# Second mixer of a two-block transformer: computed between the tiles of its input projection instead of behind it

## The reference, cut to what matters

```python
h = rmsnorm(x, mix_pre_gain)                      # 256 x 2048
proj = h @ w_in_2                                 # 2048 x 5376
q_a, k_a, v_a, q_r, f_r, i_r, g_r = split(proj)   # 1024,128,128,1024,1024,1024,1024
attn = rmsnorm(sliding_window_attention(q_a, k_a, v_a, sinks), attn_out_gain)  # 16 heads of 64, 2 key heads
f = lb + (1 - lb) * sigmoid(f_r); key = 1 - f; q = silu(q_r); v = i_r          # 8 heads of 128
b = cumsum(log f)
att[t, s] = sum_k q[t,k] key[s,k] exp(b[t,k] - b[s,k])   for s <= t
o = att @ v;  o = o * rsqrt(mean(o*o) + EPS) * norm_gain * silu(g_r)
mixed = concat(attn, o) @ w_out_2                 # 2048 x 2048
```

## Time and profile before

| | |
|---|---|
| median of 3 runs | 2506.15 us (2505.97 to 2507.98) |
| the profiled execution, time | 2511.62 us |
| its span | 2509.8 us |
| TensorE busy | 2386.6 us of the span |
| VectorE busy | 1453.9 us |
| ScalarE busy | 1155.2 us |
| mean granted TensorE clock | 0.977 of full |
| input projection of block 2 (from the span's start) | 1285.1 to 1516.1 us |
| mixer of block 2, its last transposes included | 1516.1 to 1683.8 us |
| output projection of block 2 | 1683.8 to 1771.8 us |

### The profile page before, as it was taken

The page is one execution under the profiler, slowest core; times in us unless marked ns, Lnnn a source line. Parts: engine busy times, 40 slices in busy tenths (PEclk is TensorE's granted clock), DMA queues, the critical chain, the costliest instruction groups (busy, mean ns, idle before and its releaser), DMA issues.

```text
span 2509.8 us, 34138 instructions
## 1 busy us (share of the span) xinstructions
PE 2386.6 (95%) x12062; PEld 1992.9 (79%) x12062; DVE 1453.9 (58%) x1806; ACT 1155.2 (46%) x1619; POOL 38.7 (2%) x61
## 2 busy tenths in 40 slices
PE   6999977999999999999999997869999999999997
PEld 5888856888888888888878885658888888888886
DVE  4444467557777546776554445975566544566544
ACT  4444335455555444555444445444444444444432
POOL 1000100000000000000000000000000000000000
PEclk9999878999999999999999998979999999999999
DMA  7666341646556666556666651016566666656663
GB/s 234 189 190 183 99 143 42 193 139 190 183 178 195 192 192 186 177 187 210 185 201 190 190 162 47 1 45 192 142 201 185 191 190 190 190 184 184 209 192 101
DMA packets 298804, 418.97 MB, mean 167 GB/s; under 512 B 15439, under 2 KB 181657, under 8 KB 297957
## 3 DMA queue, kind: packets, MB, share of 16 engines
q1 hardware_dynamic: 295744, 407.09, 53.2%
q0 software_dynamic: 2400, 8.68, 1.1%
q10 hardware_dynamic: 580, 2.20, 0.2%
HBM read 415.80 MB, written 2.12 MB: 167 GB/s over the span
## 4 chain that ended last, share of the span: by engine, by line
PE 80%; DVE 7%; issue 7%; ACT 2%; DMA 2%; POOL 0%; DVEq 0%; SPq 0%; POOLq 0%; ACTq 0%
PE PS L1346 22%; PE PS L1313 15%; PE PS L1314 15%; PE PS L1312 14%; PE PS L1347 11%; PE PS L1364 1%; DVE x L979 1%; DMA root_rows<-small 1%; DVE proj L1246 1%; DVE proj L1235 1%; ACT work L704 1%; DVE fackf L1242 1%; DMA stage<-in_w_in 1%; DMA root_row<-root_rows 1%; DVE work L1090 1%
## 5 line engine op out<-in xcount | busy, mean ns | idle before, releaser
L835 DVE TENSOR_TENSOR wlo<-stage,whi 128x1024 fp32r<-128x1024 f32 (+2 forms) x452 | 540.6, 1199 | 614.9 <-ACT whi L537 614.8
L1346 PE MATMUL PS<-actT,whi 128*128 128x512 f32 x2432 | 861.4, 398 | 3.0 <-DVE wlo L864 3.0
L537 ACT ACTIVATE whi<-stage 128x1024 fp32r<-128x1024 f32 (+2 forms) x452 | 468.6, 1038 | 671.1 <-PE PS L1314 646.0
L1347 PE MATMUL PS<-actT,wlo 128*128 128x256 f32 x2432 | 684.2, 281 | 0.0
L1346 PEld LDWEIGHTS PS<-actT,whi 128*128 128x128 f32 x2432 | 458.0, 188 | 116.9 <-DVE wlo L864 3.6
L864 DVE TENSOR_TENSOR wlo<-stage,whi 128x1024 fp32r<-128x1024 f32 x298 | 362.8, 1223 | 238.2 <-ACT whi L598 238.1
L598 ACT ACTIVATE whi<-stage 128x1024 fp32r<-128x1024 f32 x298 | 315.9, 1061 | 321.3 <-PE PS L1347 307.5
L1347 PEld LDWEIGHTS PS<-actT,wlo 128*128 128x128 f32 x2432 | 457.2, 188 | 0.1
L1313 PE MATMUL PS<-wlo,actT 128*128 128x512 f32 (+2 forms) x992 | 383.6, 387 | 0.0
L1312 PE MATMUL PS<-whi,actT 128*128 128x512 f32 (+2 forms) x992 | 383.6, 387 | 0.0
L1314 PE MATMUL PS<-whi,actT 128*128 128x512 f32 (+2 forms) x992 | 380.5, 384 | 0.0
(11 more groups left out here) (263 smaller groups left out, 1481.4 us busy)
## 6 DMA issues: line engine op xcount, KB each, us to landing
stage<-in_w_up SPq DMA_DIRECT2D x304, 512.0 KB, 3.9
stage<-in_w_down SPq DMA_DIRECT2D x216, 512.0 KB, 4.5
stage<-in_w_in SPq DMA_DIRECT2D x168, 512.0 KB, 4.5
stage<-in_w_out SPq DMA_DIRECT2D x64, 512.0 KB, 4.7
stage<-in_cmp_k_w SPq DMA_DIRECT2D x8, 512.0 KB, 4.6
stage<-in_cmp_v_w SPq DMA_DIRECT2D x8, 512.0 KB, 5.8
x<-in_x ACTq DMA_DIRECT2D x2, 1024.0 KB, 6.9
grow<-bias_by_distance POOLq DMA_DIRECT2D x2, 1024.0 KB, 7.5
```

The costliest lines, as they stand in the source:

```text
L537: nc.scalar.activation(whi[:, s % SPLITS, 0:wd], stage[:, s % STAGES, 0:wd], ACT.Copy)\
L835: nc.vector.tensor_tensor(wlo[:, s % SPLITS, 0:wd], stage[:, s % STAGES, 0:wd], whi[:, s % SPLITS, 0:wd].bitcast(F32), ALU.subtract).then_ ...
L1346: nc.tensor.matmul(o, whi[:, j % SPLITS, at], actT[:, k, :], start=k == 0, stop=False)
L1347: last = nc.tensor.matmul(o[:, S:2 * S], wlo[:, j % SPLITS, at], actT[:, k, 0:S], start=False, stop=k == KC - 1)
```

## The change

The 88 tiles of `in2` are written out one by one, in the order of `IN2_BLOCKS`: keys and values first, then the window queries feature-major, half of the RNN values token-major, forget gates and RNN queries feature-major in turn, then the other half of the values and the gates. 12 blocks of 4 tiles are feature-major (48 tiles), 5 token-major (40 tiles, the first 8 of them half as wide). Queries and forgets thus arrive as the transposes left them before; only the doubled keys (4 transposes) and the logarithms (two groups of 8) are still transposed.

Between these tiles stand the 16 window heads (`WINDOW_AT`, ahead of tiles 25 to 43) and the 16 steps (`STEP_AT`, ahead of tiles 57 to 82), each cut into pieces at fixed distances: on TensorE scores at n, turn at n + 2, values at n + 3; exponents at n, levels at n + 2, `att @ v` at n + 4. The projection uses PSUM banks 0 to 3, the mixer 4 to 7 (and bank 1 for `att @ v`). `qf` and `kf` get two buffers. The diagonal comes out of the level products: `keep` also takes u == t where t is the last of the lower half of a level, and the one missing corner, token 127, comes from a 32 x 32 product. `cross_out` moves from ScalarE to VectorE. The mean squares are split in two halves. The transposes for `out2` run in pairs of chunks: 4 chunks ahead of tile 87, 8 behind it, 4 between tiles 5 and 6 of `out2`, which is also written out instead of looped.

```diff
+IN2_BLOCKS = [("tok", C_KA, 256)] + [("feat", C_QA + 256 * i, 256) for i in range(4)] + [("tok", C_IR, NW)]
+for _i in range(4):
+    IN2_BLOCKS += [("feat", C_FR + 256 * _i, 256), ("feat", C_QR + 256 * _i, 256)]
+IN2_BLOCKS += [("tok", C_IR + NW, NW), ("tok", C_GR, NW), ("tok", C_GR + NW, NW)]
+IN2_BANKS = [(2 * (k % 2), 2 * (k % 2) + 1) for k in range(14)] + [(0, 3), (2, 0), (3, 2)]
+WINDOW_AT = {25 + 5 * s // 4: s for s in range(HA)}
+STEP_AT = {n: r for r, n in enumerate((57, 59, 60, 62, 63, 65, 66, 68, 72, 73, 75, 76, 78, 79, 81, 82))}
...
-        keep[:, n, :] = same & (u % (2 * ln) < ln) & (t % (2 * ln) >= ln)
+        keep[:, n, :] = same & (u % (2 * ln) < ln) & (t % (2 * ln) >= ln) | (u == t) & (t % (2 * ln) == ln - 1)
-    keep[:, 7, :] = u == t
+    keep[P - 1, 0, P - 1] = 1.0
...
 # ScalarE
+            def low_sums2(k):
+                act.wait_ge(ev("tile_used"), used(G["in2"].first + IN2_FIRST[k] + 4))
+                nc.scalar.activation(feat_dst(k), PS[:, b:b + 2, S:2 * S], ACT.Copy, ...).then_inc(ev("in2_low"), 1)
...
+            for n in range(AHEAD, IN2_TILES + AHEAD):
+                act.wait_ge(ev("tile_used"), used(G["in2"].first + n - SPLITS + 1))
+                act.wait_ge(ev(f"landed{n % STAGES}"), 16 * ((G["in2"].first + n) // STAGES + 1))
+                nc.scalar.activation(whi[:, n % SPLITS, 0:wd], stage[:, n % STAGES, 0:wd], ACT.Copy).then_inc(ev("hi_done"), 1)
...
+                ended = in2_end(n - 3)
+                if ended in FEAT_NO: low_sums2(ended)
+                if ended in TOK_NO: tokens_out(ended)
+                if n - 5 in WINDOW_AT: window_turned(WINDOW_AT[n - 5])
+                if n - 4 in WINDOW_AT: window_exp(WINDOW_AT[n - 4])
+                if n == 50: attention_squares()
+                if n - 3 in STEP_AT: decays(STEP_AT[n - 3])
+                if n - 7 in STEP_AT: o_out(STEP_AT[n - 7])
+                if n in (52, 68): sigmoids(n // 68)
+                if n in (54, 70): logs(n // 70)
+                if n in (57, 73): logs_turned(n // 73)
+                if n in (86, 90): gate_sigmoid(n // 90)
...
 # VectorE
+            def join2(k):
+                dve.wait_ge(ev("in2_low"), i + 1)
+                nc.vector.scalar_tensor_tensor(to, PS[:, b:b + 2, 0:S], ..., to, ALU.mult, ALU.add).then_inc(ev("in2_join"), 1)
+                dve.wait_ge(ev("row_in"), 32)
+                dve.wait_ge(ev("in2_join"), i + 1)
+                nc.vector.tensor_tensor(to, to, row, ALU.mult).then_inc(ev("in2_feat"), 1)
...
+            for n in range(AHEAD, IN2_TILES + AHEAD):
+                dve.wait_ge(ev("hi_done"), G["in2"].first + n + 1)
+                nc.vector.tensor_tensor(wlo[:, n % SPLITS, 0:wd], ..., ALU.subtract).then_inc(ev("lo_done"), 1)
+                if n == 7: root_of_x(3, 6)
+                if in2_end(n - 3) in FEAT_NO: join2(in2_end(n - 3))
...
+                if n - 6 in WINDOW_AT: take_out2(WINDOW_AT[n - 6])
+                if n - 4 in WINDOW_AT: weigh2(WINDOW_AT[n - 4])
+                if n - 3 in WINDOW_AT: front2(WINDOW_AT[n - 3])
+                if n in (52, 68): forgets(n // 68)
+                if n in (55, 71): keys(n // 71)
+                if n - 5 in STEP_AT: attention_levels(STEP_AT[n - 5])
+                if n - 3 in STEP_AT: products(STEP_AT[n - 3])
...
+            split_turned("mix2", range(8), MIX2_BANK)
+            gated(1)
+            split_turned("mix2", range(8, 12), MIX2_BANK)
+            tok("out2", False, then_first="up2a", beside=last_chunks)
...
 # TensorE
+            for n in range(IN2_TILES):
+                if n == 19: key_turn()
+                if n - 3 in WINDOW_AT: window_values(WINDOW_AT[n - 3])
+                if n - 2 in WINDOW_AT: window_turn(WINDOW_AT[n - 2])
+                if n in WINDOW_AT: window_scores(WINDOW_AT[n])
+                if n in (54, 70): logs_turn(n // 70)
+                if n - 4 in STEP_AT: values(STEP_AT[n - 4])
+                if n - 2 in STEP_AT: levels(STEP_AT[n - 2])
+                if n in STEP_AT: exponents(STEP_AT[n])
+                if n == IN2_TILES - 1:
+                    for p in range(2): turn_mix2(p)
+                in2_tile(n)
+            for p in range(2, 6): turn_mix2(p)
...
+            def last_turned(j):
+                if j == 6:
+                    for p in (6, 7): turn_mix2(p)
+            tok("out2", actT, turned="mix2", between=last_turned)
```

More of the change, by code:

```diff
@@ L555, in take @@
                     for t in range(TT):
[L556 to L557 removed]
+                        last = nc.scalar.activation(dst[:, t, span(col, wd)], PS[:, 4 * g.turned + 2 * bank + t, 0:wd], ACT.Copy)
                     last.then_inc(ev("acc_free"), 1)
@@ L792, in _ @@
-            decays(0)
-            for n in range(NR + 3):
-                window_turned(n)
-                if 1 <= n <= NR and (n - 1) % TT == 1:
-                    cross_out((n - 1) // TT)
-                if n >= 3:
-                    o_out(n - 3)
-                if n + 1 < NR:
-                    decays(n + 1)
-                window_exp(n)
-            first_tiles("out2")
-            act.wait_ge(ev("o_out2"), HA)
-            act.wait_ge(ev("o_out"), NR)
-            for t in range(TT):
-                last = nc.scalar.activation(squares[t][:, 0:1024], proj2[:, t, C_QA:C_QA + 1024],
-                                            ACT.Square, accum_out=small[:, t:t + 1])
@@ L808, in _, with tokens_out @@
-            last.then_inc(ev("ssq"), 1)
-            split_turned("mix2")
-            tok("out2", "squares", then_first="up2a")
+            def low_sums2(k):
+                b = IN2_BANKS[k][0]
+                act.wait_ge(ev("tile_used"), used(G["in2"].first + IN2_FIRST[k] + 4))
+                nc.scalar.activation(feat_dst(k), PS[:, b:b + 2, S:2 * S], ACT.Copy,
+                                     scale=64 ** -0.5 if FEAT_NO[k] < 4 else 1.0).then_inc(ev("in2_low"), 1)
+            def tokens_out(k):
+                act.wait_ge(ev("rstd"), 6)
+                for t in range(TT):
+                    if t == 0 and k >= 14:
+                        act.wait_ge(ev("first_half"), k - 13)
+                    else:
+                        act.wait_ge(ev("tile_used"), used(G["in2"].first + IN2_FIRST[k] + 8))
+                    nc.scalar.activation(tok_dst(k)[:, t, :], PS[:, IN2_BANKS[k][t], 0:IN2_BLOCKS[k][2]], ACT.Copy,
+                                         scale=small[:, 4 + t:5 + t]).then_inc(ev("in2_tok"), 1)
@@ L811, in _, with last_chunks @@
+            def last_chunks(j):
+                if j == 2:
+                    split_turned("mix2", range(12, KC), MIX2_BANK)
+            split_turned("mix2", range(12), MIX2_BANK)
+            tok("out2", "squares", then_first="up2a", beside=last_chunks)
             split_turned("n4")
@@ L1298, in one @@
                     for j in range(T):
+                        if between is not None and b == 0:
+                            between(j)
                         if turned is not None and b == 0:
@@ L1318, in tok @@
                     pe.wait_ge(ev("g_lo"), G[up].acc + G[up].blocks)
+                if between is not None:
+                    pairs = 0
                 if pairs:
@@ new lines, in _ @@
+            for n in range(IN2_TILES):
+                if n == 19:
+                    key_turn()
+                if n - 3 in WINDOW_AT:
+                    window_values(WINDOW_AT[n - 3])
+                if n - 2 in WINDOW_AT:
+                    window_turn(WINDOW_AT[n - 2])
+                if n in WINDOW_AT:
+                    window_scores(WINDOW_AT[n])
+                if n in (54, 70):
+                    logs_turn(n // 70)
+                if n - 4 in STEP_AT:
+                    values(STEP_AT[n - 4])
+                if n - 2 in STEP_AT:
+                    levels(STEP_AT[n - 2])
+                if n in STEP_AT:
+                    exponents(STEP_AT[n])
+                if n == IN2_TILES - 1:
+                    for p in range(2):
+                        turn_mix2(p)
+                in2_tile(n)
```

698 lines of the change are left out of this document (421 added, 277 removed).

## The result

The changed kernel takes 2495.56 us in the median of 4 runs (2494.21 to 2496.12), the kernel before beside it 2507.07 (2505.97 to 2511.18). The ratio is 0.9937, 95% interval 0.9924 to 0.9950: 11.5 us faster by the medians and 15.8 by the ratio, where 37.5 were forecast. The direction is right, and the time lies above the range. The profiled execution of after took 2494.21 us with a span of 2492.4, 17.4 less than the span before. From the first tile of `in2` (1283.9) to the last of `out2` (1754.9) it needs 471.0 us: 486.7 before, 449.2 forecast. So 21.8 us of the stage have to be found. One run of experiment 7 took 2663.81 us at a granted clock of 0.842 (its other four 2486.86 to 2495.52); it is in that kernel's median and not in its ratio.

The account below looks back on a forecast made before the run. TensorE, busy 95% of the span, was taken as the bound, the mixer being a VectorE stage between its projections. Stage: 351.8 + 97.4 = 449.2 us against 486.7, 37.5 less, giving 2469 us; range 2441 to 2492.

Parts of the forecast that it names:

- TensorE at clock 1.00 throughout: Sign expected in the profile after: TensorE keeps its full granted clock from `in2` to the end of `out2`.
- rival 3: Some 20 scattered waits drop the woven stage's clock to the mixer's mean 0.87: +51 us, kernel 2520; chance 0.05.
- a corner of 32 columns replaces the diagonal: In each step's levels, a diagonal of 32 columns instead of 128 saves about 0.1 us of TensorE.
- Ends of blocks among the heads: ScalarE's copies of finished blocks delay the heads' exp at tiles 31, 35, 39, 43: TensorE waits 2.6, 1.4, 2.0, 2.0 us.
- `exponents(2)` ahead of tile 60: TensorE waits 1.9 us for `fac`, because `decays(1)` stands behind a block's low sums on ScalarE.
- The masks at tiles 62, 65 and 81: Single PSUM level banks make `levels(r)` wait for the previous step's mask on VectorE: 1.6, 2.3 and 1.7 us.
- Tiles 67 and 68: Sigmoids and `forgets` stand ahead of masks and products of steps 4 and 5: TensorE waits 0.9 + 2.0 + 1.5 us.
- The end: Splits ready 4.8 us after tile 87, transposes filling 1.9; some 3.7 us lost at tile 6 of `out2`.
- The root row: Transfer for `join2` of the first feature block, arriving about 1313.4, stays hidden behind tiles 12 to 14 by 1.5 us.
- Rival 1: Queues absorb the waits: 21 us of waits and 6 of the end vanish, kernel 2441; chance 0.20.
- Rival 2: VectorE's order costs double, every step waiting like those at 65 to 68: 25 us more, kernel 2494; chance 0.17.
- Rival 4: Nothing comes of the change: 37 us more waits, by the root row or a starved instruction stream; chance 0.03.

Follow-up runs that it names:

- experiment 7: Changed kernel with `o_out` ahead of `decays` on ScalarE: 2490.24 us, ratio 0.9909 to the kernel before.
- experiment 5: Changed kernel with late low-sum, token and join copies, late forget gates, and earlier splits and transposes at the end: 2457.05 us, ratio 0.9784.
- Experiment 1: Changed kernel, same order, with 99 identity products of 128 x 128 filling TensorE's waits at ten places: 2482.01 us, ratio 0.9883.
- experiment 10: experiment 5 with four deliberate TensorE pauses ahead of tiles 9, 13, 17 and 21, waiting for a later tile's split: 2472.23 us, ratio 0.9846.
- experiment 6: Kernel before the change, its two long mixer pauses filled with small products (54, then 14 and 26): 2507.50 us, ratio 0.9984.
- experiment 9: experiment 5 plus one 128 x 128 product ahead of each of tiles 8 to 24, 17 in all: 2462.88 us, ratio 0.9818.
- Experiment 2: Changed kernel with `low_sums2` and `tokens_out` behind the heads' and steps' work on ScalarE, `join2` behind `front2` on VectorE: 2479.17 us, ratio 0.9871.
- experiment 3: Changed kernel with `forgets` at n = 52 and 68 behind `attention_levels` and `products` on VectorE: 2490.54 us, ratio 0.9913.
- Experiment 4: Changed kernel with the first 4 chunks split during tile 87, last transposes ahead of `out2` tile 5, their split two tiles later: 2485.18 us, ratio 0.9889.
- 8: experiment 5 plus `o_out` ahead of `decays` on ScalarE: 2459.92 us, ratio 0.9791.

## Why the prediction was wrong

The stage, as TensorE spends it, in us. The columns of after and of experiment 5 add up, by line, the time from the start of each product to the start of the next, less the waits.

| | forecast | after | experiment 5 |
|---|---|---|---|
| 48 feature-major tiles | 135.8 | 145.9 | 138.3 |
| 40 token-major tiles | 99.1 | 103.7 | 103.5 |
| 16 heads and 16 steps | 92.8 | 99.2 | 93.5 |
| transposes | 5.9 | 5.9 | 5.4 |
| `out2` | 88.0 | 89.7 | 88.1 |
| waits | 27.6 | 26.5 | 6.7 |

The forecast column adds up to 449.2 (its steps' waits, named one by one, to 12.3 where the sum has 12.4), the last one to 435.5, and the trace of experiment 5 has 1723.1 - 1287.5 = 435.6. That of after adds up to 470.9 for 471.0.

**The step that failed** is "TensorE at clock 1.00 throughout", and the sentence behind it in rival 3: "the old loop idled 12% in pieces and kept 1.00; the clock fell where idle time was 17.6 of 28 us; my longest wait is under 5". I priced each wait at its length. The pieces of the old loop were 0.5 and 0.8 us long, as the one in the earlier trace rows; mine were 1 to 6. Waits of 1.07, 1.81, 2.14 and 2.47 us were each followed by 1.2 GHz. What it cost is the difference between the last two columns without the waits: 7.6 + 0.2 + 5.7 + 0.5 + 1.6 = 15.6 us. Experiment 1, with the order unchanged, shows 15.9 less in the same rows (428.5) and won 13.6 by filling the same waits; experiment 10 shows the mechanism alone. Rival 3 was the right mechanism with a size too large: 34.1 us of low clock are 0.07 of the stage, not the 0.26 taken from the mixer's mean, and before and after differ little in low time (44.4 and 34.1 us). What differs is what TensorE does in it. Before, it is mostly idle (experiment 6: 34 us less of it are worth 4); after, it is dense work.

The Trainium skill ("TensorE: Matmul & The Clock Gate", A second HAM failure mode) says that short idle times between groups of products let the clock swing between its two levels. Experiment 1 agrees. The page has the median product at its full-clock duration and puts the loss between the bursts; here most products keep theirs too, but those in the stretches take 0.64 us a pair, and the loss lies in them.

**The term that was too small** is TensorE's own work at full clock: 138.3 + 103.5 + 93.5 in experiment 5 against 135.8 + 99.1 + 92.8, 7.6 us. The prediction named it ("if the woven groups cost more TensorE time beside fp32r tiles than among themselves") and took nothing for it. By the starts some 5.1 us of it stand on the first fp32r product behind each of 54 groups, 0.08 to 0.12 a time; experiment 9 shows that this is the end of the last float32 pass and not yet a price of mixing. What can be read is inside a group. The prediction took 0.1 off a step because a corner of 32 columns replaces the diagonal. Levels, corner (line 1818) and the next exponents in experiment 5:

```profile
1478.41 1.72 PE L1815 MATMUL PS<-win 128*128 128x128 f32 x14
1480.07 0.25 PE L1818 MATMUL PS<-QRT,FRT 128*32 128x32 f32 x2
1480.25 1.12 PE L1801 MATMUL PS<-grow,logf 128*128 128x512 f32 x2
1481.21 0.81 PE L1802 MATMUL PS<-grow,logf 128*128 128x384 f32 x2
```

Levels and corner take 1480.25 - 1478.41 = 1.84 us, and the pair of exponents behind the corner 0.96 instead of 0.86 (1484.90 to 1485.76, the next exponents, which stand behind an fp32r tile): together 1.94 against 1.79 for levels and diagonal in the prediction. The corner costs 0.15 more where 0.1 less was forecast: 0.25 x 16 = 4.0 us. The 8 half-wide tiles took 11.6 instead of 11.1. The other 3.1 us stay open. All of this is read from traces; no run isolates the corner.

Together 15.6 + 7.6 - 0.4 (transposes and `out2`) - 1.1 (waits) is 21.7, the difference of the two columns. The medians differ less than the profiled pair, 11.5 against 17.4 us: the profiled execution before lay 4.5 over its median, that of after 1.4 under.

**The waits, place by place.**
- Ends of blocks among the heads, 8.0 forecast: 2.47 + 1.07 + 1.81 + 1.81 = 7.2. Experiment 2 removed all by the order of the copies, so their cause is right.
- `exponents(2)` ahead of tile 60, 1.9: 1.60, and gone with the low sums. Right.
- The masks at tiles 62, 65 and 81, 5.6 in all: only 0.77, at 62. In their place stand 2.14 at tile 64 and 2.37 at tile 80, ahead of `att @ v`. I had the chain over the mask and its single banks; the one that ended last was `o_out` of the step before, queued on ScalarE behind `decays`. Experiment 7 shows it, by what went and by what came. That the steps' waits still add up, 12.8 for 12.4, is in part luck.
- Tiles 67 and 68, 4.4: 5.95 at 67. The start is as forecast (`forgets` ahead of masks and products, experiment 3), the way to TensorE again over `o_out`. ScalarE and VectorE of after:

```profile
1545.96 1.28 ACT L862 ACT_TABLE_LOAD   x1 [5.40 <-DVE win L1351]
1547.25 1.02 ACT L862 ACTIVATE win<-PS 128x1024 f32<-128x1024 f32 x1
1548.17 0.27 ACT L867 ACTIVATE logf<-PS 128x128 f32<-128x128 f32 x1
1548.33 0.29 ACT L868 ACTIVATE PS<-PS 128x128 f32<-128x128 f32 x1
```

```profile
1539.96 1.38 DVE L1303 TENSOR_SCALAR FRT<-FRT,lbs 128x256 f32<-128x256 f32 x4
1541.26 1.08 DVE L1363 TENSOR_TENSOR win<-PS,grow 128x896 f32<-128x896 f32 x1
...
1543.64 1.22 DVE L1344 TENSOR_TENSOR win<-win,QRT 128x1024 f32<-128x1024 f32 x1
1544.77 1.08 DVE L1351 TENSOR_TENSOR win<-win,FRT 128x896 f32<-128x896 f32 x1
```

  ScalarE stands in `decays(6)` until VectorE has the products of step 5, loads the table, takes the exp, and only then reaches the `o_out` that TensorE waits for. The table load is on the path here, 1.28 of the 5.95: it came after ScalarE's wait, not in it as in the earlier trace rows. The Trainium skill ("ScalarE: Activation LUTs", What ACT_TABLE_LOAD costs) has a drain beside the load; none stands in these rows either.
- The end, 2.9 and 3.7: 3.03 and 3.52. Experiment 4 removed both.
- The root row, hidden by 1.5 us: hidden. VectorE waited 4.86 us for it, and TensorE not at all:

```profile
1312.93 0.69 DVE L1279 TENSOR_TENSOR win<-win,root_row 128x512 f32<-128x512 f32 x1 [4.86 <-DMA root_row<-root_rows]
```

**The rivals.** Rival 1 (the queues absorb the waits, 2441) did not hold for this order, but experiment 5 comes near it by another order: 2457, short by 6.7 us of waits and 7.6 of TensorE's own time. Rival 2 gives 2494 and so nearly the measured time, by a mechanism that did not happen: VectorE's order did not cost double. Without experiments the time alone would have spoken for it. Rival 4 is out.

## What to carry to other kernels

A wait of 1 to 6 us in a dense stream of TensorE has to be priced at its length and at what may then be done at 1.2 GHz: here seven of eleven places were followed by a low stretch, at about 2 us each (15.6 in all), and removing 8.8 us of waits won 16.6. When independent work is woven between tiles, the copies that nobody waits for go behind the work that TensorE waits for, in every queue; here that order (experiments 2 and 3) and the earlier end were worth more than twice the change itself. Low clock is a cost only where TensorE has work: compare not how much there is, but what lies in it.

## What the runs showed of the hardware

- At seven of the eleven places where TensorE waits in the changed kernel the granted clock was 0.5 for 3.41 or 6.83 us; at the others, one of them 3.03 us long, it stayed at 1.00. The same wait of 1.63 us was followed by a low stretch in experiments 9 and 10 and not in 2, 5 and 8. The length of a pause alone does not tell.
- Two pauses of 1.15 us among fp32r tiles left the clock at 1.00, one of 2.40 brought 3.41 us at 1.2 GHz, one of 5.23 brought 6.83.
- A float32 product of 128 x 128 between fp32r products costs 0.21 us of TensorE, 0.14 to the next start and 0.08 on the fp32r product behind it; among others of its kind its two passes take 0.22 (14 of them from 1596.53 to 1598.10).
- A float32 product of 32 x 32 ahead of the next exponents cost 0.15 us more than one of 128 x 128 in its place (1.94 against 1.79).
- Adding 99 products of 128 x 128 in waits made the program 13.6 us faster.

Open is what decides whether a pause brings the clock down, and 3.1 us of TensorE's own work.
